# A second block's MLP up projection in channel order with the weights stationary, and two reordered places: the first chunk and the state-space roots

## The chip, the cores and the metric

The kernel runs on one core of a Trainium2 chip. The metric is device time in microseconds (us) from launch to the end of one execution; three runs of the kernel before gave 3005.98, 3007.11 and 3009.41, median 3007.11. About 0.2% (6 us) is the least difference that can be told from none.

The core has a matrix engine (PE; its weight loads are listed apart as PEld), a vector engine (DVE), an activation engine (ACT), GpSimd (POOL) and a queue engine (SP) that here issues the weight loads from memory. They run on their own and meet at semaphores.

## The reference, cut to what matters

256 tokens, width 2048, two blocks in fp32. The three places that the change touches:

```
proj = rmsnorm(h, g) @ w_in                       # first block: its first 512 columns are the "first chunk"
...
y = _ssd(...) + d_skip * xs;  y = y * silu(z)     # state space, 4 groups of 512 channels
y_ssm = rmsnorm(y.reshape(b, s, 4, 512), ssm_norm_g)   # one root per token and group
h = h + concat([y_ssm, y_att]) @ w_out
...
h = rms_norm(x, g_mlp)                            # second block's MLP, hidden width 8192
x = x + jnp.square(relu(h @ w_mlp_up)) @ w_mlp_down
return rms_norm(x, g_final)
```

The root 1/rms of a token is a positive factor r of its whole row, so square(relu(r * u)) is r * r * square(relu(u)).

## The kernel before, in words

**Weights.** All large products run through one stream of weights. A slab is 256 input rows by 512 output columns (two tiles of 128 x 512, 512 KB). SP loads slabs in order into a ring of four (`w_raw`); ACT rounds each to `w_hi` (fp32r, line 754), DVE forms the rest `w_lo = w_raw - w_hi` (line 1341). `hi_ready` and `lo_ready` count slabs; SP reloads a place once its `w_lo` is written, ACT overwrites `w_hi` once PE has counted the slab of four before in `slab_done`. Four slabs are a quad; `split(q, a, b)` on ACT and on DVE does slabs a to b of quad q.

**Products.** The activations are kept as channels x tokens, also in two parts (`a_hi`, `a_lo`; for the MLP's second product `m_hi`, `m_lo`). A 128x128 tile of them is the stationary operand, 512 weight columns are the moving one, and the result is 128 tokens x 512 columns in a bank of PSUM. A slab takes 12 matmuls of 512 columns: hi x hi, lo x hi (line 2137) and hi x lo (line 2142), for two weight tiles and two token tiles. A chunk is 512 output columns over all 2048 inputs: 8 slabs.

**Operands.** A new operand is turned on PE (line 2165, four 128x128 transposes per pair of channel tiles), rounded by ACT (`gained`, line 779, or `rounded_operand`, line 773) and its rest formed by DVE (`gained_rest`, line 1355, `rest_of_operand`, line 1347). The engines' orders are written out by hand: each block below is one engine's program.

**First chunk.** `first_chunk` on PE turns tile pairs 0 and 1, then for slab s turns pair s+1, waits for `a_lo` of pair s and runs slab s. ACT does pair s+1 ahead of the rounding of slab s (line 845 on). After the chunk comes `narrow`: 48 matmuls whose stationary operand has 32 columns and whose moving operand has 256 (lines 2213 to 2215). It waits for DVE's line 1469, which follows eight squares of ACT (line 763) and one small rounding (line 856).

**State-space groups.** In a loop over four groups POOL scales (lines 614 to 629), PE multiplies within and across chunks beside the slabs of the q, k, v chunks, and DVE makes the gated output in `z`. After the loop POOL computes all eight roots `ssm_rs` (lines 547, 548) and DVE normalizes `z` (line 1611); PE turns it beside the last chunk of q, k, v, in groups of pairs (0,1), (2), (3,4), (5), (6) ahead of slabs 3 to 7.

**MLP.** `w_mlp_up` is taken in 16 blocks of 512 hidden channels. Per block PE runs the up chunk of block j+1 into the banks of `pair[2]`, then `mlp_down` of block j (four chunks of two slabs). ACT and DVE scale the up chunk's result by r into `m_stage` (lines 784 and 1361), PE turns it to channel order (`mlp_channels`, line 2234, eight transposes into banks 6 and 7), ACT takes relu and its square (`m_relu` line 1277, `m_hi` line 1280), DVE the exact product `m_act` (line 2049) and the rest `m_lo` (line 2055), and DVE adds each down chunk to `h` (line 1413). The last block's relu to `m_lo` (lines 1299, 1301, 2084, 2088) stands between the last transposes and the last down product.

Of the kernel before, what the change touches and what calls it, by code (L numbers as in the profile page):

```python
# [192 lines left out]
def program(nc, wstream, small, const, out):  # L193

    ctx = ExitStack()
    with ctx:
# [27 lines left out]
        with ExitStack() as rows:  # L224
# [55 lines left out]
            with ExitStack() as part:  # L280
# [255 lines left out]
        def _(pool):  # L536
# [66 lines left out]
            for g in range(GROUPS):  # L603
# [22 lines left out]
                for t in range(TT):  # L626
# [3 lines left out]
                    if t == 0:  # L630
# [6 lines left out]
            inverse_root(ssm_rs[:].rearrange("p t g -> p (t g)"), ssm_ss[:].rearrange("p t g -> p (t g)"),  # L637
                         TT * GROUPS, 1.0 / NC, EPS, ssm_rstd)
# [108 lines left out]
        def _(act):  # L747
# [103 lines left out]
            split(Q_XBC + 1, QUAD - 1, QUAD)  # L851
# [2017 lines left out]
```

## Time and profile before

| | before |
|---|---|
| median of three runs | 3007.11 us |
| the profiled execution | 3011.07 us, its span 3009.0 us |
| PE busy | 2955.5 us, 98% |
| PEld busy | 2422.7 us, 81% |
| DVE busy | 2010.2 us, 67% |
| ACT busy | 1411.7 us, 47% |
| POOL busy | 322.5 us, 11% |
| mean granted clock of TensorE | 0.994 |

The page of the profile lists busy time per engine, the chain of work that ended last, and groups of instructions by line. The timeline lists instructions in order of time with their start, length and, in brackets, how long the engine had been idle and what released it.
### The profile page before, as it was taken

To read this page: it belongs to the slowest core of one execution; us is meant where nothing else is said; L and a number is where in the kernel's file an instruction comes from. 1 tells how busy PE (TensorE), PEld (TensorE's weight loads), DVE (VectorE), ACT (ScalarE), POOL (GpSimd) and SP (SyncE) were. 2 spreads that over 40 slices of the span, in tenths; PEclk is the share of its full clock that TensorE was granted. 3 is DMA by queue.
4 is the path that set the end of the run, shared out by engine and by line. 5 is a ranking of instruction groups with operands and counts; after the bars stand their busy time and mean duration, and the time that the engine had idled before them with its cause. 6 is when DMAs were issued, how large, how long until landed. Compare 5 with 4: busy or idle time off the path is not lost.

```text
span 3009.0 us, 43769 instructions
## 1 busy us (share of the span) xinstructions
PE 2955.5 (98%) x15191; PEld 2422.7 (81%) x15191; DVE 2010.2 (67%) x2615; ACT 1411.7 (47%) x1807; POOL 322.5 (11%) x276
## 2 busy tenths in 40 slices
PE   6999999999999999999999999999999999999998
PEld 5888877788888888887878877777888888888886
DVE  3765777756666777776668677777655666666665
ACT  4444445644444444445554554333545444444444
POOL 0001880000000000000000054443000000000000
PEclk8999999999999999999999999999999999999999
DMA  4555444456555555564565533333765565555554
GB/s 167 181 183 188 136 135 150 134 187 217 189 188 188 184 188 181 187 196 146 183 230 179 168 126 126 113 124 112 240 220 193 185 196 188 187 190 188 188 189 140
DMA packets 145142, 525.73 MB, mean 175 GB/s; under 512 B 16416, under 2 KB 17184, under 8 KB 144160
## 3 DMA queue, kind: packets, MB, share of 16 engines
q1 hardware_dynamic: 139760, 503.72, 51.6%
q0 software_dynamic: 1536, 11.78, 1.1%
q10 hardware_dynamic: 3760, 9.05, 0.9%
q8 instruction: 58, 0.95, 0.1%
q14 instruction: 28, 0.23, 0.0%
HBM read 516.09 MB, written 8.39 MB: 174 GB/s over the span
## 4 chain that ended last, share of the span: by engine, by line
PE 91%; DVE 3%; issue 2%; ACT 2%; POOL 1%; DMA 1%; DVEq 0%; ACTq 0%; POOLq 0%; SPq 0%
PE bank L2137 55%; PE bank L2142 27%; PE bank L2234 1%; DVE w_lo L1341 1%; ACT w_hi L754 1%; PE bank L2554 1%; PE bank L2165 1%; DMA w_raw<-weights 1%; PE bank L2583 0%; PE bank L2372 0%; PE bank L2305 0%; PE bank L2466 0%; PE bank L2316 0%; PE bank L2242 0%; DVE delta L1875 0%
## 5 line engine op out<-in xcount | busy, mean ns | idle before, releaser
L1341 DVE TENSOR_TENSOR w_lo<-w_raw,w_hi 128x1024 fp32r<-128x1024 f32 x952 | 1197.3, 1267 | 789.5 <-ACT w_hi L754 788.3
L754 ACT CAST w_hi<-w_raw 128x1024 fp32r<-128x1024 f32 x952 | 1000.1, 1052 | 1408.7 <-PE bank L2142 1394.9
L2137 PE MATMUL bank<-w_hi,a_hi 128*128 128x512 f32 x2816 | 1125.5, 400 | 16.5 <-ACT w_hi L754 14.6
L2137 PE MATMUL bank<-w_hi,a_lo 128*128 128x512 f32 x2816 | 1104.2, 392 | 0.0
L2142 PE MATMUL bank<-w_lo,a_hi 128*128 128x512 f32 x2816 | 761.4, 391 | 0.0
L2137 PEld LDWEIGHTS bank<-w_hi,a_hi 128*128 128x128 f32 x2816 | 531.8, 189 | 136.0 <-DVE a_lo L1355 13.0
L2142 PEld LDWEIGHTS bank<-w_lo,a_hi 128*128 128x128 f32 x2816 | 531.7, 189 | 112.8
L2137 PEld LDWEIGHTS bank<-w_hi,a_lo 128*128 128x128 f32 x2816 | 532.6, 189 | 107.1 <-issue 1.9
L2137 PE MATMUL bank<-w_hi,m_hi 128*128 128x512 f32 x496 | 193.5, 390 | 2.3 <-issue 2.3
L2137 PE MATMUL bank<-w_hi,m_lo 128*128 128x512 f32 x496 | 193.4, 390 | 0.0
L1413 DVE TENSOR_TENSOR h<-h,bank 128x512 f32<-128x512 f32 x236 | 151.1, 682 | 19.6 <-PE bank L2142 19.5
L2137 PE MATMUL bank<-w_hi,f_hi 128*128 128x512 f32 x352 | 138.8, 394 | 0.0
L553 POOL TENSOR_TENSOR rstd<-rstd,neg_half 128x2 f32<-128x2 f32 x6 | 4.8, 798 | 1240.9 <-DVE rstd L1370 1240.9
L2137 PE MATMUL bank<-w_hi,f_lo 128*128 128x512 f32 x352 | 137.1, 390 | 0.0
L2142 PE MATMUL bank<-w_lo,m_hi 128*128 128x512 f32 x496 | 133.5, 391 | 0.0
L2137 PEld LDWEIGHTS bank<-w_hi,m_hi 128*128 128x128 f32 x496 | 93.4, 188 | 21.9 <-issue 2.5
L2142 PEld LDWEIGHTS bank<-w_lo,m_hi 128*128 128x128 f32 x496 | 93.7, 189 | 19.6
L2137 PEld LDWEIGHTS bank<-w_hi,m_lo 128*128 128x128 f32 x496 | 93.4, 188 | 19.4
L2142 PE MATMUL bank<-w_lo,f_hi 128*128 128x512 f32 x352 | 94.2, 389 | 0.0
L2142 PEld LDWEIGHTS bank<-w_lo,f_hi 128*128 128x128 f32 x352 | 66.1, 188 | 13.9
L2137 PEld LDWEIGHTS bank<-w_hi,f_lo 128*128 128x128 f32 x352 | 66.1, 188 | 13.5 <-issue 0.2
L745 POOL TENSOR_TENSOR rstd<-rstd,neg_half 128x1 f32<-128x1 f32 x2 | 1.5, 746 | 704.6 <-DVE rstd L2099 704.6
(397 smaller groups left out, 2489.7 us busy)
## 6 DMA issues: line engine op xcount, KB each, us to landing
w_raw<-weights SPq DMA_DIRECT2D x952, 512.0 KB, 4.1
gate<-gate_st ACTq DMA_DIRECT2D x8, 512.0 KB, 3.9
h<-gate ACTq DMA_DIRECT2D x8, 512.0 KB, 4.7
gain<-gains POOLq DMA_DIRECT2D x3, 1024.0 KB, 6.9
h<-x_tok SPq DMA_DIRECT2D x4, 512.0 KB, 11.1
w_proj_sb<-w_proj POOLq DMA_DIRECT2D x1, 2048.0 KB, 9.8
h_rest<-h POOLq DMA_DIRECT2D x1, 2048.0 KB, 13.2
h<-h_rest POOLq DMA_DIRECT2D x1, 2048.0 KB, 9.6
```

The lines of the kernel that those rows point to most:

```text
L553: nc.gpsimd.tensor_tensor(rstd[:, n], rstd[:, n], neg_half[:, 0:TT], ALU.pow).then_inc(rstd_ready, 1)
L745: nc.gpsimd.tensor_tensor(rstd[:, N_OUT, t:t + 1], rstd[:, N_OUT, t:t + 1], neg_half[:, 0:1], ALU.pow).then_inc(rstd_ready, 1)
L754: nc.scalar.copy(w_hi[:, s, :], w_raw[:, s, :]).then_inc(hi_ready, 1)
L1341: V.tensor_tensor(w_lo[:, s, :], w_raw[:, s, :], w_hi[:, s, :].bitcast(F32), ALU.subtract).then_inc(lo_ready, 1)
L1413: V.tensor_tensor(h[:, t, col], h[:, t, col], pair[p][t][:], ALU.add).then_inc(pair_free[p], 1)
L2137: T.matmul(psum[t][:], left[:, t * P:(t + 1) * P], wh, start=start and j == 0 and n == 0, stop=False)
L2142: last = T.matmul(psum[t][:], products[j][0][:, t * P:(t + 1) * P], wl, start=False, stop=stop and j == SLAB_KT - 1)
L2165: last = T.transpose(bank[4 + i % 4][:, k * SEQ + t * P:k * SEQ + (t + 1) * P], src[:, t, (2 * i + k) * P:(2 * i + k + 1) * P], ident[:])
L2234: last = T.transpose(bank[first + ct // 2][:, (ct % 2) * SEQ + t * P:(ct % 2) * SEQ + (t + 1) * P], src[:, t, col0 + ct * P:col0 + (ct + 1 ...
L2554: last = T.matmul(out[r, r], left[:, r], right[:, r], start=True, stop=True)
```

## The change

It has three parts.

**First chunk.** ACT rounds slab s ahead of tile pair s+1, not behind it, and DVE's `gained_rest` follows suit. PE's order stays. ACT's order in this part before, from the first rounding of an operand (`a_hi`; `gain_col_sb` holds the norm's gains) on:

```order
L779 ACTIVATE a_hi<-bank,gain_col_sb 128x256 [waits tr_ready,gain_ready]
L779 ACTIVATE a_hi<-bank,gain_col_sb 128x256
L779 ACTIVATE a_hi<-bank,gain_col_sb 128x256 [waits tr_ready]
L779 ACTIVATE a_hi<-bank,gain_col_sb 128x256
L754 CAST w_hi<-w_raw 128x1024 [waits raw_loaded0]
L779 ACTIVATE a_hi<-bank,gain_col_sb 128x256 [waits tr_ready]
L779 ACTIVATE a_hi<-bank,gain_col_sb 128x256
L754 CAST w_hi<-w_raw 128x1024 [waits raw_loaded1]
```

The same place in the changed kernel:

```order
L782 ACTIVATE a_hi<-bank,gain_col_sb 128x256 [waits tr_ready,gain_ready]
L782 ACTIVATE a_hi<-bank,gain_col_sb 128x256
L757 CAST w_hi<-w_raw 128x1024 [waits raw_loaded0]
L782 ACTIVATE a_hi<-bank,gain_col_sb 128x256 [waits tr_ready]
L782 ACTIVATE a_hi<-bank,gain_col_sb 128x256
L757 CAST w_hi<-w_raw 128x1024 [waits raw_loaded1]
```

The rounding of slab 1 (`raw_loaded1`) stood behind the third tile pair and now stands behind the second.

**State-space roots.** POOL computes group g-1's two roots inside the loop at group g, between `xds` and the skip product; DVE normalizes group g-1 there. After the loop only group 3 is left, and PE turns one pair ahead of each of slabs 1 to 7. DVE's order behind the loop before (`z` is what is normalized, `a_lo` the rest of an operand, `w_lo` the rest of a slab):

```order
L1572 TENSOR_REDUCE qk_ss<-xs 128x8 [waits qk_sq] x2
L1611 SCALAR_TENSOR_TENSOR z<-z,ssm_rs,gain 128x512 [waits gain_loaded,ssm_rstd]
L1611 SCALAR_TENSOR_TENSOR z<-z,ssm_rs,gain 128x512
L1341 TENSOR_TENSOR w_lo<-w_raw,w_hi 128x1024 [waits hi_ready]
L1611 SCALAR_TENSOR_TENSOR z<-z,ssm_rs,gain 128x512 x2
L1341 TENSOR_TENSOR w_lo<-w_raw,w_hi 128x1024 [waits hi_ready]
L1611 SCALAR_TENSOR_TENSOR z<-z,ssm_rs,gain 128x512 x2
L1341 TENSOR_TENSOR w_lo<-w_raw,w_hi 128x1024 [waits hi_ready]
L1611 SCALAR_TENSOR_TENSOR z<-z,ssm_rs,gain 128x512 x2
L1347 TENSOR_TENSOR a_lo<-bank,a_hi 128x512 [waits a_hi_ready] x3
```

The same place now:

```order
L1575 TENSOR_REDUCE qk_ss<-xs 128x8 [waits qk_sq] x2
L1568 SCALAR_TENSOR_TENSOR z<-z,ssm_rs,gain 128x512 [waits ssm_rstd]
L1568 SCALAR_TENSOR_TENSOR z<-z,ssm_rs,gain 128x512
L1343 TENSOR_TENSOR a_lo<-bank,a_hi 128x512 [waits a_hi_ready]
L1337 TENSOR_TENSOR w_lo<-w_raw,w_hi 128x1024 [waits hi_ready]
L1343 TENSOR_TENSOR a_lo<-bank,a_hi 128x512 [waits a_hi_ready]
L1337 TENSOR_TENSOR w_lo<-w_raw,w_hi 128x1024 [waits hi_ready]
```

Six of the eight normalizing instructions left this place for the loop, two in each of groups 1 to 3.

**MLP.** The up chunk is computed with 128x128 tiles of the weights stationary and 256 tokens moving (`channel_chunk`), so it comes out in channel order. `m_stage` and `mlp_channels` are gone; relu reads banks 6 and 7 (for block 0 `pair[0]`) without r, and `ms_m` = r * r is applied where the down product is added to `h`. The relu of block j+1 moves to the end of its up chunk; the last block gets buffers of its own (`last_hi`, `last_lo`). PE's order at the end of a block before, where a down slab ends and the next block's up chunk begins:

```order
L2142 MATMUL bank<-w_lo,m_hi 128x512 [waits lo_ready]
L2142 MATMUL bank<-w_lo,m_hi 128x512 x3
L2234 MATMUL bank<-ident_sb,m_stage 128x128 [waits pair_free2]
L2234 MATMUL bank<-ident_sb,m_stage 128x128 x7
L2764 UNCONDITIONAL_BRANCH
L2764 ISA
L2132 ISA [waits pair_free2]
L2137 MATMUL bank<-w_hi,a_hi 128x512 [waits hi_ready]
L2137 MATMUL bank<-w_hi,a_lo 128x512
```

PE's order now, from the end of an up chunk to the start of the down product:

```order
L2735 MATMUL bank<-a_hi,w_hi 128x256
L2736 MATMUL bank<-a_lo,w_hi 128x256
L2739 MATMUL bank<-a_hi,w_lo 128x256 [waits lo_ready]
L2739 MATMUL bank<-a_hi,w_lo 128x256 x7
L2753 ISA [waits ff_lo]
L2117 ISA [waits pair_free0]
L2122 MATMUL bank<-w_hi,m_hi 128x512 [waits hi_ready]
L2122 MATMUL bank<-w_hi,m_lo 128x512
```

A slab of the up projection is 24 matmuls of 256 columns in place of 12 of 512, each with a weight load of 128 columns; the transposes are gone.

```diff
@@ ACT, first chunk @@
+            split(0, 0, 1, first=True)
+            for s in range(1, QUAD):
+                gained(TR_ATTN, C_ATTN, s)
+                split(0, s, s + 1, first=True)
             for s in range(QUAD):
-                gained(TR_ATTN, C_ATTN, s + 1)
-                split(0, s, s + 1, first=True)
-            for s in range(QUAD - 1):
-                gained(TR_ATTN, C_ATTN, QUAD + s + 1)
+                gained(TR_ATTN, C_ATTN, QUAD + s)
                 split(Q_XBC + 1, s, s + 1)
@@ POOL, in the loop over groups @@
                     pool.wait_ge(y_squared, TT * g)
+                    inverse_root(ssm_rs[:, :, g - 1], ssm_ss[:, :, g - 1], TT, 1.0 / NC, EPS, ssm_rstd)
@@ DVE, in the loop over groups @@
+                if g:
+                    ssm_normalize(g - 1)
@@ PE, last chunk of q, k, v @@
-                  between={3: lambda: tiles_of_y(0, 1), 4: lambda: tiles_of_y(2), 5: lambda: tiles_of_y(3, 4),
-                           6: lambda: tiles_of_y(5), 7: lambda: tiles_of_y(6)})
+                  between={i + 1: lambda i=i: tiles_of_y(i) for i in range(KT // 2 - 1)})
@@ PE, MLP @@
+            def channel_chunk(q, psum, ahead=None):
+                for n in range(KT // SLAB_KT):
+                    if ahead:
+                        ahead(n)
+                    u, s = q + n // QUAD, n % QUAD
+                    first, final = n == 0, n == KT // SLAB_KT - 1
+                    places = [(j, ct, psum[ct // 2][:, (ct % 2) * SEQ:(ct % 2 + 1) * SEQ], slice(j * NC + ct * P, j * NC + (ct + 1) * P))
+                              for j in range(SLAB_KT) for ct in range(NC // P)]
+                    pe.wait_ge(hi_ready, QUAD * u + s + 1)
+                    for j, ct, o, w in places:
+                        T.matmul(o, w_hi[:, s, w], a_hi[:, n * SLAB_KT + j], start=first and j == 0 and ct % 2 == 0, stop=False)
+                        T.matmul(o, w_hi[:, s, w], a_lo[:, n * SLAB_KT + j], start=False, stop=False)
+                    pe.wait_ge(lo_ready, QUAD * u + s + 1)
+                    for j, ct, o, w in places:
+                        last = T.matmul(o, w_lo[:, s, w], a_hi[:, n * SLAB_KT + j], start=False,
+                                        stop=final and j == SLAB_KT - 1 and ct % 2 == 1)
+                    last.then_inc(slab_done, 1)
...
             def mlp_block(j, between=None):
                 q = Q_MLP + 2 + 4 * j
-                chunk(q, 2, V_MLP + j, a_hi, a_lo, between=between)
+                channel_chunk(q, bank[6:8])
                 pe.wait_ge(ff_lo, N_FF + 2 * j + 2)
                 mlp_down(q + 2, U_MLP + 2 * j)
-                pe.wait_ge(pair_free[2], 2 * (V_MLP + j + 2))
-                mlp_channels()
@@ DVE, MLP @@
+            def add_block_to_h(p, col, tiles=range(TT)):
+                for t in tiles:
+                    V.scalar_tensor_tensor(h[:, t, col], pair[p][t][:], ms_m[:, t:t + 1], h[:, t, col], ALU.mult, ALU.add).then_inc(pair_free[p], 1)
```

## Rows read from the trace of the kernel before

**Rows 1.** The page: span, busy time by engine, chain that ended last by line.

```profile
span 3009.0 us, 43769 instructions
PE 2955.5 (98%) x15191; PEld 2422.7 (81%) x15191; DVE 2010.2 (67%) x2615; ACT 1411.7 (47%) x1807; POOL 322.5 (11%) x276
...
PE bank L2137 55%; PE bank L2142 27%; PE bank L2234 1%; DVE w_lo L1341 1%; ACT w_hi L754 1%; PE bank L2554 1%; PE bank L2165 1%; DMA w_raw<-weights 1%; PE bank L2583 0%; PE bank L2372 0%; PE bank L2305 0%; PE bank L2466 0%; PE bank L2316 0%; PE bank L2242 0%; DVE delta L1875 0%
```

**Rows 2.** Stretches: length, PE, PEld, DVE, ACT, POOL busy, clock, DMA share, GB/s.

```profile
16.50:59.50 43.00, 31.27 (x109) 23.87 (x107) 13.74 (x19) 16.32 (x35) 0.00 (x0) 0.80 0.35 118
...
46.98:50.39 3.41, 3.39 (x8) 2.73 (x9) 1.13 (x1) 0.00 (x0) 0.00 (x0) 0.50 0.34 91
...
2311.00:2348.00 37.00, 37.00 (x165) 30.65 (x164) 22.14 (x24) 15.35 (x15) 0.00 (x0) 1.00 0.61 186
```

**Rows 3.** Timeline, first chunk: start, length, engine, line, operation, idle before.

```profile
16.55 0.60 PE L2165 MATMUL bank<-ident_sb,h 128*128 128x128 f32 x4
17.19 0.84 ACT L779 ACTIVATE a_hi<-bank,gain_col_sb 128x256 fp32r<-128x256 f32 x2 [5.82 <-PE bank L2165]
17.92 1.04 ACT L754 CAST w_hi<-w_raw 128x1024 fp32r<-128x1024 f32 x1
...
19.11 0.47 PE L2137 MATMUL bank<-w_hi,a_hi 128*128 128x512 f32 x1 [1.95 <-ACT w_hi L754]
...
51.41 0.60 PE L2165 MATMUL bank<-ident_sb,h 128*128 128x128 f32 x4
...
60.96 0.31 PE L2213 MATMUL bank<-a_hi,w_hi 128*32 128x256 f32 x1 [1.31 <-DVE w_lo L1469]
```

**Rows 4.** DMA: first four slabs (issue line 493) to landing; all sixteen until 75 us.

```profile
L493 SPq DMA_DIRECT2D w_raw<-weights x4: 424/616/672, 1.5 to 4.0; - x4
...
DMA to landing us min/median/max: 8.8/10.0/11.3
...
w_raw<-weights SPq DMA_DIRECT2D x16, 512.0 KB, 4.3
```

**Rows 5.** Timeline of PE, last chunk of q, k, v beside the turned y.

```profile
424.14 1.07 PE L2142 MATMUL bank<-w_lo,a_hi 128*128 128x512 f32 x4
...
441.66 0.63 PE L2165 MATMUL bank<-ident_sb,z 128*128 128x128 f32 x4 [2.60 <-DVE a_lo L1347]
...
449.66 0.60 PE L2165 MATMUL bank<-ident_sb,z 128*128 128x128 f32 x4
...
452.85 0.60 PE L2165 MATMUL bank<-ident_sb,z 128*128 128x128 f32 x4
```

**Rows 6.** Timeline: PE at group 2 of the state space; a root of width 2 on POOL.

```profile
364.85 1.12 PE L2324 MATMUL bank<-work,b_tok 128*128 128x512 f32 x2 [0.95 <-POOL work L618]
...
2296.22 0.72 POOL L553 TENSOR_TENSOR rstd<-rstd,neg_half 128x2 f32<-128x2 f32 x1 [100.79 <-DVE rstd L1370]
```

**Rows 7.** Timeline of PE around the MLP's transposes: first, a middle and the last block.

```profile
2305.98 1.07 PE L2142 MATMUL bank<-w_lo,a_hi 128*128 128x512 f32 x4
...
2308.61 0.39 PE L2137 MATMUL bank<-w_hi,a_lo 128*128 128x512 f32 x1
...
2348.30 1.08 PE L2142 MATMUL bank<-w_lo,m_hi 128*128 128x512 f32 x4
...
2350.33 0.39 PE L2137 MATMUL bank<-w_hi,a_lo 128*128 128x512 f32 x1
...
2970.29 1.08 PE L2142 MATMUL bank<-w_lo,m_hi 128*128 128x512 f32 x4
...
2978.82 0.49 PE L2137 MATMUL bank<-w_hi,m_hi 128*128 128x512 f32 x1
```

**Rows 8.** Other shapes: the end of `narrow`; state-space matmuls 128x128; their weight loads.

```profile
66.47 0.28 PE L2215 MATMUL bank<-a_lo,w_hi 128*32 128x256 f32 x1
...
297.40 1.95 PE L2305 MATMUL bank<-before_sb,cv 128*128 128x128 f32 x16
...
L2305 PEld LDWEIGHTS bank<-before_sb,cv x128: 188/192/192, 297.2 to 405.7; 128*128 128x128 f32 x128
```

More of the change, by code:

```diff
@@ L1294, in _ @@
                 split(q + 4)
-            act.wait_ge(ff_t, N_FF + N_FF2)
+            with act.Fori(0, N_FF2 - 2) as j:
+                mlp_block(j)
+            mlp_block(N_FF2 - 2, last=True)
             j = N_FF2 - 1
-            for b in range(2):
-                half = slice(2 * b, 2 * b + 2)
-                nc.scalar.activation(m_relu[:, half].rearrange("p k s -> p (k s)"), bank[6 + b][:], ACT.Relu).then_inc(ff_silu, 1)
-                act.wait_ge(ff_silu, N_FF + 2 * j + b + 1)
-                nc.scalar.activation(m_hi[:, half], m_relu[:, half], ACT.Square).then_inc(ff_hi, 1)
@@ L2054, in mlp_gated, with mlp_down @@
                     dve.wait_ge(ff_hi, N_FF + 2 * j + b + 1)
-                    V.tensor_tensor(m_lo[:, half], m_act[:, half], m_hi[:, half].bitcast(F32), ALU.subtract).then_inc(ff_lo, 1)
-            def mlp_down(q, chunks=range(D // NC)):
-                for n in chunks:
+                    V.tensor_tensor(lo[:, half], m_act[:, half], hi[:, half].bitcast(F32), ALU.subtract).then_inc(ff_lo, 1)
+            def mlp_down(q):
+                for n in range(D // NC):
                     split(q + 1 + n // 2, 2 * (n % 2), 2 * (n % 2) + 2)
@@ L2089, in _ @@
-            mlp_down(N_QUADS - 4, range(D // NC - 1, D // NC))
+                dve.wait_ge(ff_lo, N_FF + 2 * j + 2)
+                mlp_act(j + 1, bank[6:8])
+                if last:
+                    mlp_lo(j + 1, last_hi, last_lo)
+                mlp_down(q + 2)
+            with dve.Fori(0, N_FF2 - 2) as j:
+                mlp_block(j)
+            mlp_block(N_FF2 - 2, last=True)
             def out_gain(t, n):
@@ L2771, in _ @@
                     pe.wait_ge(ff_lo, N_FF + 2 * (N_FF2 - 1) + s + 1)
-                    slab(N_QUADS - 2, 2 * n + s, [(m_hi[:, 2 * s + k], m_lo[:, 2 * s + k]) for k in range(SLAB_KT)],
+                    slab(N_QUADS - 2, 2 * n + s, [(last_hi[:, 2 * s + k], last_lo[:, 2 * s + k]) for k in range(SLAB_KT)],
                          pair[n], s == 0, s == 1)
@@ L2782, in _ @@
                             wh, wl = (x[:, i, k * NC:(k + 1) * NC] for x in (w_hi, w_lo))
-                            T.matmul(pair[n % 2][t][:], m_hi[:, tile, ts], wh, start=tile == 0, stop=False)
-                            T.matmul(pair[n % 2][t][:], m_lo[:, tile, ts], wh, start=False, stop=False)
-                            last = T.matmul(pair[n % 2][t][:], m_hi[:, tile, ts], wl, start=False, stop=tile == 3)
+                            T.matmul(pair[n % 2][t][:], last_hi[:, tile, ts], wh, start=tile == 0, stop=False)
+                            T.matmul(pair[n % 2][t][:], last_lo[:, tile, ts], wh, start=False, stop=False)
+                            last = T.matmul(pair[n % 2][t][:], last_hi[:, tile, ts], wl, start=False, stop=tile == 3)
                         last.then_inc(slab_done, 1)
```

143 lines of the change are left out of this document (59 added, 84 removed).

## The prediction

> **What bounds the kernel now.** I read the page first: PE is busy 98% of the span and the lines of the large products (2137 and 2142) are 82% of the chain that ended last [rows 1]. So PE's own pace decides, and a gain can only be a PE instruction removed, a faster one, or one of the few places where PE stands still. Then the stretches: in the MLP PE is full and DVE and ACT are at 22.1 and 15.4 of 37 us; 165 matmuls are listed in 37.00 us, of which two may hang over an edge, so a matmul of 512 columns takes 0.227 us and a slab of twelve 2.72 us. In the first chunk the granted clock is 0.80 in the mean, and one stretch of 3.41 us at 0.50 holds only 8 matmuls, 0.427 each [rows 2]. Last the timelines of PE at the three places that the change touches; the rows give where PE idles and what comes last there.
>
> **First chunk.** PE turns tile pair 2 at 16.55; ACT then does pair 2 (17.19) and only behind it slab 1's rounding (17.92), and PE starts slab 1 at 19.11, idle 1.95 us for that rounding [rows 3]. The same wait of about 2 us comes at slabs 1 to 7, and part of each slab runs at the lower clock. With the new order slab s is rounded before PE has turned pair s+1, so PE goes on at once. Beside it ACT needs 0.84 + 1.04 us per slab [rows 3], much less than PE. A slab with four transposes ahead takes 452.85 - 449.66 = 3.19 us at full clock [rows 5]. Pair 7 would be turned at 16.55 + 5 x 3.19 = 32.5 instead of 51.41. From there to `narrow` it took 60.96 - 51.41 = 9.55 us [rows 3], a chain on ACT and DVE that is unchanged but for one rounding (1.0) that now lies ahead of pair 7: 8.5, so `narrow` starts at 41.0, 19.9 earlier. What is late next is this chain: PE ends slab 7 at 16.55 + 6 x 3.19 + 2.72 = 38.4 and idles 2.6 us, not 1.3. Idling 1.31 us there cost no clock; 1.95 us at the slabs did. A stretch at 0.50 does half its 3.41 us of work, 1.7 us; I take half of that, 0.8. The data are there: the first four slabs, issued by 4.0 us, land within 11.3 us of issue, before 16; a later one lands some 4.3 us after issue [rows 4] and is asked for three slabs (9.6 us) ahead. Result -19.1, between -15 (the clock still falls twice, one landing late) and -19.9.
>
> **State-space roots.** PE ends slab 0 at 424.14 + 4 x 0.227 = 425.05 and turns pair 7 at 452.85 [rows 5]; in between it waits for the normalized `z`, once 2.60 us for the rest of an operand, and runs a stretch at the lower clock. With one pair turned ahead of each of slabs 1 to 7, pair 7 comes at 425.05 + 7 x 3.19 = 447.4: -5.5. DVE's rests and slabs (two short instructions a slab) fit in 3.19 us. The price is in the loop: POOL gets a root of width 2, 0.72 us [rows 6], and a scaling with its hand-over of some 0.3, three times. In group 2 PE already waits 0.95 us for POOL [rows 6], so there POOL's 1.0 us is on the path; in groups 1 and 3 POOL itself waits for DVE later. Cost 1.0, between 0 and 3. The six normalizing instructions in the loop are hidden by DVE's waits for ACT's roundings. Result -4.5, between -2.5 and -5.5.
>
> **MLP, what is removed.** In block 0, PE's last slab before the transposes ends with 4 matmuls from 2305.98; the second matmul after them should start 5 x 0.227 later, at 2307.11, and starts at 2308.61: 1.50. In a middle block 2350.33 - (2348.30 + 1.13) = 0.90, 14 times: 12.6. At the last block the first matmul of the second down slab would come at 2970.29 + 16 x 0.227 = 2973.92 and comes at 2978.82: 4.90, the wait for relu to `m_lo` with the lower clock behind it [rows 7]. With `last_hi` that work lies beside the previous down product. Sum -19.0. In return no wait is added that PE reaches: relu of block j+1 ends some microseconds after its up chunk, and its banks are needed again only after a down product of eight slabs. DVE's adds gain a factor but keep their shape, and each of ACT and DVE loses an instruction per block; with DVE busy 22.1 of 37 us [rows 2] this is hidden. If that cover were gone, DVE's two products ahead of the down product's slabs would cost PE up to 1.3 us a block.
>
> **MLP, what is added.** 16 up chunks of 96 matmuls of 512 columns become 16 x 192 = 3072 of 256, and 1536 more weight loads of 128 columns. The trace has no such matmul with such a load. The nearest rows: `narrow`, the same type and 256 moving columns, but loads of 32: 48 matmuls from 60.96 to 66.47, 5.51 / 47 = 0.1172 each [rows 3, 8]. And the state-space products, where loads of 128 columns and 128x128 matmuls run at (1.95 - 0.28) / 15 = 0.111 (0.28 is the listed length of a last one, as at 66.47) although each load is listed with 0.192 [rows 8]: the listed length is no pace, and a load needs at most 0.111. I take the larger of the two paces, 0.1172: (2 x 0.1172 - 0.2267) x 1536 = +11.9. Ends: half the old pace, 0.1133, gives 0; the listed 0.192 as a pace gives +230.
>
> The Trainium skill (TensorE: Matmul & The Clock Gate, section Back-to-back issue gap) puts a lone matmul at N / 2.4 + 2.5 ns; 256 columns would be 109 ns, against 216 for 512, and the doubling would cost about 4 us. The trace does not agree: 117 and 227 ns.
>
> **Sum.** -19.1 - 4.5 - 19.0 + 11.9 = -30.7. The profiled execution took 3011.07 (span 3009.0 and 2.1 around it), 4.0 over the median of the runs: 2980.4 on its scale, 2976.4 on the median's. Forecast 2976.
>
> **Rivals.**
>
> Slower: the load is not hidden under a matmul of 256 columns. A 512-column matmul lasts long enough to cover a load; a 256-column one lasts about as long as the load, and if the load had to wait for the matmul's end, 1536 more loads at 0.111 would stand in the open: +170 in place of +11.9, 3135. The kernel gets slower from a pace of 0.1172 + 30.7 / 3072 = 0.127 on. For it: nothing in the trace shows both at once in fp32r. Against: `before_sb,cv` runs load and matmul of nearly equal length at 0.111, so they overlap [rows 8]. Chance 6%. The Trainium skill (same page, section The mechanism) says that a load overlaps a matmul in flight only when the two use different row groups, which speaks for this rival; the trace disagrees, as loads of all 128 rows run beside matmuls of all rows.
>
> A dearer pace: what a 256-column matmul takes beyond 256 / 2.4 GHz = 0.1067, namely 0.0105 [rows 3, 8], comes on top of the load's 0.111: 0.1215, so +25 in place of +11.9: 2990. For it: load and matmul are near a tie. Against: at the tie in `before_sb,cv` nothing is added. Chance 15%.
>
> The first chunk gives half: the clock falls in stretches as now (0.80 in the mean) or ACT's order makes another wait. For it: the clock before 16 us is low, and PE idles before `narrow`. Against: no idle is left between slabs. -9.5 in place of -19.1: 2986. Chance 11%.
>
> A cheaper pace: 256 columns cost half of 512, 0.1133: 2964.5. For it: the weight load is hidden in both. Against: `narrow`. Chance 6%.
>
> The change does nothing: the removed waits come back at the next wait of each place. Against: the waits are for work that is off PE, and PE is full behind each. About 3%.
>
> **How the numbers follow.** My forecast has 59%, own range 2969 to 2984. The range that should hold 8 in 10 reaches from the cheaper pace to the dearer one with a small loss elsewhere: 2965 to 2994. About 0.2% (6 us) is what can be told from no change; slower by that needs the first rival, 6%; within it are the last rival and one in a hundred of the others, 4%; faster 90%.
>
> **What would show each step.** First chunk: no wait of PE for `w_hi` after slab 0, `narrow` starting near 41, clock near 1.00 from 16 us on; wrong if slabs stay 5 us or more apart. Roots: PE turns `z` four transposes at a time every 3.19 us without a wait, and the wait for POOL in group 2 grows by about 1. MLP: up slabs of 24 matmuls in 2.81 us; a block period of 21.8 + 22.5 = 44.3 us, against 22.5 + 21.8 + 0.90 = 44.4 before; no gap at the last block. If an up slab takes over 3.05 us, the gain is gone.

## The result, and the profile after

The changed kernel took 2991.41 us, the median of five runs (2990.52 to 2995.49), for 3007.11 before: a ratio of 0.9949, 95% interval 0.9934 to 0.9963. The gain of 15.7 us is clear of the noise and is half of the 30.7 forecast; 2991.4 lies in the range, and is close to the 2990 of the rival "a dearer pace". The profiled execution took 2991.41, with a span of 2989.6 for 3009.0 before. The profiled execution of the kernel before was 4.0 over its median and that of the changed kernel is its median, so the traces differ by some 4 us more than the medians do.

The page of the changed kernel (span; busy time by engine; the chain that ended last, by line), which answers to [rows 1]:

```profile
span 2989.6 us, 46565 instructions
PE 2949.5 (99%) x16599; PEld 2481.6 (83%) x16599; DVE 2008.3 (67%) x2600; ACT 1402.6 (47%) x1791; POOL 327.3 (11%) x282
PE bank L2122 46%; PE bank L2127 23%; PE bank L2739 4%; PE bank L2736 4%; PE bank L2735 4%; DVE w_lo L1337 1%; PE bank L2219 1%; PE bank L2538 1%; PE bank L2150 1%; ACT w_hi L757 1%; DMA w_raw<-weights 1%; POOL work L633 1%; PE bank L2567 0%; PE bank L2356 0%; POOL xs L601 0%
```

PE still bounds the kernel. The new lines 2735, 2736 and 2739 are the up projection in channel order. Next PE's timeline of the changed kernel (start, length, line, what, idle before it and its releaser), in the first chunk and at the turned `z`, for [rows 3, 5]:

```profile
16.47 0.60 PE L2150 MATMUL bank<-ident_sb,h 128*128 128x128 f32 x4
19.67 0.60 PE L2150 MATMUL bank<-ident_sb,h 128*128 128x128 f32 x4
...
32.48 0.60 PE L2150 MATMUL bank<-ident_sb,h 128*128 128x128 f32 x4
...
41.08 0.31 PE L2198 MATMUL bank<-a_hi,w_hi 128*32 128x256 f32 x1 [2.51 <-DVE w_lo L1463]
...
407.73 0.60 PE L2150 MATMUL bank<-ident_sb,z 128*128 128x128 f32 x4
...
430.03 0.60 PE L2150 MATMUL bank<-ident_sb,z 128*128 128x128 f32 x4
...
434.36 0.63 PE L2341 MATMUL bank<-ident_sb,qkv 128*128 128x128 f32 x4 [0.99 <-DVE a_lo L1343]
```

Slabs with their transposes come every 3.20 us without a wait, pair 7 at 32.48 (forecast 32.5), `narrow` at 41.08 (41.0). Pair 7 of `z` follows pair 0 by 22.30, seven times 3.19. The stretches of the changed kernel (length; PE, PEld, DVE, ACT, POOL busy; clock, DMA share, GB/s) answer to [rows 2]:

```profile
16.50:42.00 25.50, 22.99 (x117) 18.81 (x116) 14.46 (x27) 17.76 (x37) 1.24 (x1) 1.00 0.59 206
...
2330.00:2351.00 21.00, 21.00 (x177) 21.00 (x177) 11.58 (x12) 8.63 (x10) 0.00 (x0) 1.00 0.58 189
```

The clock is full in the first chunk, where it was 0.80. In the up chunk the loads (PEld) are busy all 21.00 us, as the matmuls are: a thing that no row of before showed. The timeline of PE there, an up chunk between two down products, and the start of the last down product, for [rows 7]:

```profile
2329.00 0.28 PE L2735 MATMUL bank<-a_hi,w_hi 128*128 128x256 f32 x1
2329.12 0.28 PE L2736 MATMUL bank<-a_lo,w_hi 128*128 128x256 f32 x1
2329.24 0.28 PE L2735 MATMUL bank<-a_hi,w_hi 128*128 128x256 f32 x1
...
2330.92 1.12 PE L2739 MATMUL bank<-a_hi,w_lo 128*128 128x256 f32 x8
2331.88 0.28 PE L2735 MATMUL bank<-a_hi,w_hi 128*128 128x256 f32 x1
...
2348.20 1.12 PE L2739 MATMUL bank<-a_hi,w_lo 128*128 128x256 f32 x8
...
2352.04 0.40 PE L2122 MATMUL bank<-w_hi,m_hi 128*128 128x512 f32 x1
...
2955.58 1.07 PE L2127 MATMUL bank<-w_lo,m_hi 128*128 128x512 f32 x4
2956.48 0.39 PE L2122 MATMUL bank<-w_hi,last_hi 128*128 128x512 f32 x1
```

Every matmul of the up chunk starts 0.1200 us after the one before it: a slab of 24 takes 2.88, a chunk of 192 takes 2352.04 - 2329.00 = 23.04. The forecast had 0.1172, 2.81 and 22.5. Before, chunk and transposes took 22.66. At the last block the wait is gone.

To see where the rest went I cut the traces at the starts of the same matmuls, from the first transpose of `h` to PE's last matmul, and took each stretch's length less that of the kernel before. The labels e2 to e10 are the experiments below (e10 leaves out half of the up projection). One stretch of 3.41 us at the half clock (granted clock 0.50) costs up to 1.7, and such stretches come and go between executions, so a lone difference of 1.3 to 1.7 that another kernel shows without its cause is put down to them. In the fourth column no kernel changes anything but the first three up slabs (+0.5 with the channel order), yet it reads +0.5 to +3.7: half-clock stretches and waits between 1545 and 1790 us differ from one execution to the next.

| us, less before | to `narrow` | to `b_tok`, group 2 | to pairs of q, k, v | to the last pair of the MLP's operand | to the first down | 14 blocks | last but one down, to the last | last down | sum |
|---|---|---|---|---|---|---|---|---|---|
| after | -19.9 | +0.4 | -3.0 | +1.7 | +0.5 | +5.5 | -3.3 | -1.6 | -19.6 |
| e2 token MLP | -19.4 | +1.8 | -3.0 | +0.7 | 0.0 | 0.0 | 0.0 | 0.0 | -19.8 |
| e3 channel MLP | +0.6 | -0.1 | -1.6 | +2.5 | +0.5 | +5.5 | -3.3 | -1.6 | +2.6 |
| e4 early last | -20.4 | +0.5 | -3.0 | +3.1 | 0.0 | 0.0 | -0.4 | -1.7 | -21.9 |
| e5 first chunk | -19.7 | 0.0 | -0.1 | +1.5 | 0.0 | 0.0 | 0.0 | -1.6 | -19.8 |
| e6 roots | +0.2 | +0.5 | -3.0 | +2.1 | 0.0 | 0.0 | 0.0 | -1.6 | -1.7 |
| e7 root later | -20.2 | +2.4 | -4.3 | +0.5 | 0.0 | 0.0 | -0.4 | -1.7 | -23.6 |
| e8 add first | -20.4 | +0.6 | -3.0 | +1.0 | 0.0 | 0.0 | -2.4 | -1.7 | -25.9 |
| e9 both | -20.0 | +2.5 | -4.2 | +0.7 | 0.0 | 0.0 | -2.4 | -1.7 | -25.1 |
| e10 half | -19.2 | +1.9 | -3.2 | +3.7 | -1.5 | -12.2 | -3.3 | -1.6 | -35.5 |

### The profile page after: what moved, and what is told of

Its sections match the earlier page's. It is cut to its first block, busy times and chain, and to the rows that moved or that the text cites. A ratio compares the mean times of both kernels' runs of the same rounds, so it can differ in the third digit from the quotient of the medians.

```text
span 2989.6 us, 46565 instructions
## 1 busy us (share of the span) xinstructions
PE 2949.5 (99%) x16599; PEld 2481.6 (83%) x16599; DVE 2008.3 (67%) x2600; ACT 1402.6 (47%) x1791; POOL 327.3 (11%) x282
## 3 DMA queue, kind: packets, MB, share of 16 engines
q0 software_dynamic: 1536, 11.78, 1.1%
## 4 chain that ended last, share of the span: by engine, by line
PE 89%; POOL 3%; DVE 3%; issue 2%; ACT 2%; DMA 1%; DVEq 0%; ACTq 0%; SPq 0%; POOLq 0%
PE bank L2122 46%; PE bank L2127 23%; PE bank L2739 4%; PE bank L2736 4%; PE bank L2735 4%; DVE w_lo L1337 1%; PE bank L2219 1%; PE bank L2538 1%; PE bank L2150 1%; ACT w_hi L757 1%; DMA w_raw<-weights 1%; POOL work L633 1%; PE bank L2567 0%; PE bank L2356 0%; POOL xs L601 0%
## 5 line engine op out<-in xcount | busy, mean ns | idle before, releaser
L2122 PE MATMUL bank<-w_hi,a_hi 128*128 128x512 f32 x2304 | 921.1, 400 | 4.7 <-ACT w_hi L757 2.8
L2122 PE MATMUL bank<-w_hi,a_lo 128*128 128x512 f32 x2304 | 900.1, 391 | 0.0
L2127 PE MATMUL bank<-w_lo,a_hi 128*128 128x512 f32 x2304 | 622.0, 390 | 0.0
L2127 PEld LDWEIGHTS bank<-w_lo,a_hi 128*128 128x128 f32 x2304 | 433.2, 188 | 91.5
L2736 PE MATMUL bank<-a_lo,w_hi 128*128 128x256 f32 x1024 | 251.2, 283 | 0.0
L2735 PE MATMUL bank<-a_hi,w_hi 128*128 128x256 f32 x1024 | 251.2, 283 | 0.0
L2736 PEld LDWEIGHTS bank<-a_lo,w_hi 128*128 128x128 f32 x1024 | 196.5, 192 | 0.6
L2735 PEld LDWEIGHTS bank<-a_hi,w_hi 128*128 128x128 f32 x1024 | 196.5, 192 | 0.6
L2739 PE MATMUL bank<-a_hi,w_lo 128*128 128x256 f32 x1024 | 143.7, 283 | 0.0
L2739 PEld LDWEIGHTS bank<-a_hi,w_lo 128*128 128x128 f32 x1024 | 132.1, 192 | 0.0
```

The source lines that it names most:

```text
L2122: T.matmul(psum[t][:], left[:, t * P:(t + 1) * P], wh, start=start and j == 0 and n == 0, stop=False)
L2127: last = T.matmul(psum[t][:], products[j][0][:, t * P:(t + 1) * P], wl, start=False, stop=stop and j == SLAB_KT - 1)
L2735: T.matmul(o, w_hi[:, s, w], a_hi[:, n * SLAB_KT + j], start=first and j == 0 and ct % 2 == 0, stop=False)
L2736: T.matmul(o, w_hi[:, s, w], a_lo[:, n * SLAB_KT + j], start=False, stop=False)
L2739: last = T.matmul(o, w_lo[:, s, w], a_hi[:, n * SLAB_KT + j], start=False, stop=final and j == SLAB_KT - 1 and ct % 2 == 1)
```

## The experiments

Each code cut shows the main lines only. Those of e2 and e10 are against the changed kernel, that of e4 against e2, those of e7 and e8 against e4.

### e1: the pace of a matmul by itself

Nineteen bursts of 96 fp32r matmuls, each of this form, with m stationary and n moving columns (m also sets the number of rows of the result):

```
+ for i in range(N):
+     b, o = places(kind, n)[i % len(places(kind, n))]
+     last = T.matmul(bank[b][0:m, o], stationary(kind, i, m), a_hi[:, i % 2, 0:n], start=False, stop=False)
```

> This kernel leaves the whole computation out: it loads x, and TensorE runs 19 bursts of 96 fp32r matmuls, twice over, each burst with its own number of stationary columns (32 to 128), moving columns (128 to 512) and places in PSUM. Read is the time from one start to the next within a burst. Theory (a matmul of this kind costs its columns and a fixed part): the changed kernel showed 120.0 ns for 256 columns and 226.7 for 512, both behind a load of 128 columns, which is 0.417 ns a column and 13.3 ns fixed; so 384 columns take 173, 192 take 93, and 128 columns are bound by the load at 108 to 112 (the transposes' spacing). First rival (the length of the load sets the part on top): 256 columns behind 32 stationary columns take 117.3 as in the narrow projection, 64 and 96 lie between, 512 behind 32 take less than 226.7. Second rival (where the result goes sets it: half a bank, the same place twice, changing banks): behind 128 stationary columns the bursts of 256 columns with other places in PSUM differ by 2 ns or more among themselves, and the one that stays in one place of one bank takes 117 or less. The theory gives them all 120.0.

Each row below is one burst: count, length of a matmul, start of the first and of the last. The pace is the difference of the two over 95. The form at the end gives the stationary columns (128*128, 128*96, ...) and the moving ones.

```profile
L75 PE MATMUL bank<-a_hi,w_hi x96: 389/389/389, 47.7 to 69.2; 128*128 128x512 f32 x96
...
L79 PE MATMUL bank<-a_hi,w_hi x96: 333/334/346, 69.4 to 85.9; 128*128 128x384 f32 x96
...
L87 PE MATMUL bank<-a_hi,w_hi x96: 283/283/283, 97.6 to 109.0; 128*128 128x256 f32 x96
...
L107 PE MATMUL bank<-a_hi,w_hi x96: 244/275/277, 154.4 to 164.9; 128*128 128x128 f32 x96
...
L111 PE MATMUL bank<-a_hi,w_hi x96: 274/278/307, 165.1 to 176.1; 128*96 128x256 f32 x96
...
L115 PE MATMUL bank<-a_hi,w_hi x96: 276/276/276, 176.2 to 187.0; 128*64 128x256 f32 x96
...
L119 PE MATMUL bank<-a_hi,w_hi x96: 276/276/276, 187.1 to 197.9; 128*32 128x256 f32 x96
...
L135 PE MATMUL bank<-a_hi,w_hi x96: 220/222/224, 258.9 to 264.6; 128*64 128x128 f32 x96
...
L147 PE MATMUL bank<-a_hi,w_hi x96: 283/283/283, 282.0 to 293.4; 128*128 128x256 f32 x96
```

From the exact starts: 256 moving columns take 120.0 ns behind 128 stationary columns, 116.3 behind 96, 113.3 behind 64 and behind 32. The place in PSUM makes no difference: one place, two halves of a bank, two banks, four places, eight banks (line 147) and the same weights each time all give 119.9 to 120.0, and the kernel's own order, two matmuls in turn on one place, 120.5. Behind 128 stationary columns 512 moving ones take 226.7, 384 take 173.6, 192 take 111.5 and 128 take 111.3; 128 behind 64 take 60.0.

So the number of stationary columns matters, as the first rival says, and the theory of a fixed part of 13.3 falls, since with a short load 256 columns take 6.7 less; so does the second rival. A load of 128 columns paces PE at 111 ns, a stream of 256 columns at 113.3, and the two together give not the larger but 120.0. With 384 columns nothing is left of it: 173.4 behind 32, 173.6 behind 128. The first rival was wrong in detail: 117.3 behind 32 columns, taken from `narrow` [rows 8], came out as 113.3, the same as behind 64, and 512 behind 32 took 231.7 (behind 64: 229.9) and not less than 226.7. Neither has been explained. A burst with fewer stationary columns also writes fewer rows of the result, so the length of the load is not told apart from that; for the load speaks that at 384 moving columns both give the same.

### e2: the token-order MLP with the two reordered places

```
-            channel_chunk(Q_MLP, pair[0], late_tiles)
+            late_chunk(TR_MLP, h_chunk(U_WO2), Q_MLP, 0, U_MLP)
...
-                channel_chunk(q, bank[6:8])
+                chunk(q, 2, V_MLP + j, a_hi, a_lo, between=between)
                 pe.wait_ge(ff_lo, N_FF + 2 * j + 2)
                 mlp_down(q + 2, U_MLP + 2 * j)
+                pe.wait_ge(pair_free[2], 2 * (V_MLP + j + 2))
+                mlp_channels()
```

> The changed kernel with the MLP of the kernel before, that is, the first chunk and the state-space roots changed and nothing else. Theory (the MLP change is what came out dearer than forecast, by the pace of 0.1200 us for a matmul of 256 columns): the MLP begins 21.2 us earlier than in the kernel before, as in the changed kernel, and then takes as long as in the kernel before: 3007.1 - 21.2 = 2985.9, so 5 to 6 us faster than the changed kernel; blocks every 44.43 us. Rival (the first chunk and the roots gave less than is seen, and the MLP gave the forecast -7.1): 2991 + 7 = 2998.

2988.35 (2986.46 to 2991.22), ratio to the kernel before 0.9930 (0.9916 to 0.9943). The kernel before took 3009.2 beside it, so the gain is 20.8, as the theory had it (21.2), where the rival had 9. The changed kernel's own ratio, 0.9949 (0.9934 to 0.9963), overlaps with it; the table tells them apart in the MLP's columns, where e2 has 0.0 and the changed kernel +1.2, with 0.5 more in the column ahead of them (the first three up slabs, 72 matmuls).

### e3: the channel-order MLP alone

The eight pieces of the diff in the MLP, without those in the first chunk and at the roots.

> The kernel before with the MLP change alone. Theory (pace 0.1200): the ends read from the two traces, block 0 with the first chunk +1.0, 14 blocks of 44.82 for 44.43 = +5.5, the last block -4.9, together +1.6: 3008.7, no difference that the timing can tell. Forecast's own terms C and D: -7.1, 3000.0. Rival (what comes before the MLP interacts with it, so that the parts do not add): neither, and the first chunk or the middle of the trace differs from that of the kernel before by over 0.5 us.

3012.32 (3008.09 to 3013.36), ratio 1.0007 (0.9998 to 1.0016): no gain, and perhaps a small loss. In the trace its MLP columns equal those of the changed kernel to 0.01: +0.5, +5.5, -3.3, -1.6. The last of these need not be the MLP's, since e5 and e6 show it too. So the MLP change costs about 0.5 + 0.5 + 5.5 - 3.3 = +3.2 (+1.6 if the 1.6 is counted to it), where the forecast had -7.1. The last column is the half-clock stretch behind the wait before the last down product: it stands in two of the four traces with that wait (the kernel before and e2) and in none of the seven without it, so what its removal is worth lies between 0 and 1.6.

### e4: token order, and the last operand early

```
-                mlp_down(q + 2, U_MLP + 2 * j)
-                pe.wait_ge(pair_free[2], 2 * (V_MLP + j + 2))
-                mlp_channels()
+                mlp_down(q + 2, U_MLP + 2 * j, turned if last else None)   # turned(): that wait and the transposes
+                if not last:
+                    turned()
...
+                if last:                     # ScalarE, ahead of its splits of the down slabs
+                    mlp_relu(j + 1, last_hi)
...
-            mlp_down(N_QUADS - 4, range(D // NC - 1))
+            mlp_down(N_QUADS - 4, range(1))
+            mlp_gated(N_FF2 - 1, last_hi, last_lo)
+            mlp_down(N_QUADS - 4, range(1, D // NC))
```

> As the run with the token-order MLP, and the operand of the last block is turned, squared and split into buffers of its own while the down projection of the block before it runs (its transposes stand between the first and the second of the four column pairs there). Theory (the last block's gain in the changed kernel comes from this early operand and not from the channel order): the wait of 2.54 us before the last down projection goes, and with it the half clock that followed it, together -4.0 against the token-order run: 2981.9, the fastest of all. Rival (without the channel order the operand is late, since it needs transposes and a staging copy as well): TensorE stands in the down projection of the last block but one or ahead of the last, and the time is that of the token-order run, 2986, or above.

2988.81 (2987.07 to 2991.15), ratio 0.9931 (0.9918 to 0.9945), the same as e2 within the noise: a miss. In the trace its end is 2.1 shorter than e2's, and 1.7 of that is the half-clock stretch that e2 has and e4 has not; the fourth column took 2.4 more. The wait before the last down product is gone, and a new one stands in the down product before it. The timeline of e4, all engines:

```profile
2935.85 1.09 ACT L1272 ACTIVATE m_relu<-bank 128x512 f32<-128x512 f32 x2 [4.63 <-PE bank L2215]
2936.82 1.15 ACT L1275 ACTIVATE last_hi<-m_relu 128x512 fp32r<-128x512 f32 x2
2937.87 2.94 ACT L756 CAST w_hi<-w_raw 128x1024 fp32r<-128x1024 f32 x3
2938.95 2.36 DVE L1336 TENSOR_TENSOR w_lo<-w_raw,w_hi 128x1024 fp32r<-128x1024 f32 x2 [6.39 <-ACT w_hi L756]
...
2941.22 1.28 DVE L1408 TENSOR_TENSOR h<-h,bank 128x512 f32<-128x512 f32 x2
...
2942.56 0.50 PE L2118 MATMUL bank<-w_hi,m_hi 128*128 128x512 f32 x1 [1.26 <-DVE h L1408]
```

DVE stands 6.39 us for `w_hi`, which ACT rounds only behind relu and square, and DVE's addition to `h` stands in its queue behind that. PE needs the bank that this addition frees, and stands idle 1.26 us.

### e5 and e6: the first chunk alone, the roots alone

The two pieces of the diff in the first chunk; the six at the roots.

> The kernel before with the first chunk's change alone. Forecast's term A: -19.1. The two traces together gave -19.5 behind the narrow projection (41.08 us for 60.96, less 0.4 lost further on). Theory (the parts add): 3007.1 - 19.5 = 2987.6, the narrow projection begins at 41.1, and the half-clock stretches in the first 50 us are gone. Rival (what the first chunk wins is lost again in the state-space stretch, where GpSimd is as late as TensorE): -17 or less gained, 2990 or above, with new waits for GpSimd between 300 and 400 us.

2991.09 (2990.07 to 2995.45), ratio 0.9944 (0.9930 to 0.9958): 17.7 for 19.5 expected, within the interval. The time alone would also suit the rival (2990 or above); the trace decides. `narrow` begins at 41.2, and at the matmul of group 2 shown below (345.11 for 364.85) all of it is still there, with the old wait of 0.95 and no new one. The rival falls.

> The kernel before with the state-space roots' change alone. Forecast's term B: -4.5. The two traces together gave -3.0 (-22.4 at 600 us, less -19.5). Theory (parts add): 3004.1; the last pair of z is turned 4.5 to 5.5 us earlier relative to what stands before it, and 1.5 is lost to the root in group 2. Rival (the GpSimd wait belongs to the earlier arrival from the first chunk, not to the root): -4.5 or more, 3002.6 or below, and no new wait in groups 1 to 3.

3008.26 (3004.24 to 3011.47), ratio 0.9996 (0.9987 to 1.0005): by the timing no difference. In the trace +0.5 - 3.0 = -2.5, and 1.6 of that is a half-clock stretch of the kernel before that e3, with the old roots and the old waits, has not got. What the roots bring is then 0.9 where that stretch does not come and 2.5 where it does. The new wait for GpSimd is there without the new first chunk, so it belongs to the root. PE at `b_tok` in groups 2 and 3, of e5 (roots as before) and of e6 (new):

```profile
345.11 1.12 PE L2322 MATMUL bank<-work,b_tok 128*128 128x512 f32 x2 [0.95 <-POOL work L618]
376.16 1.13 PE L2322 MATMUL bank<-work,b_tok 128*128 128x512 f32 x2
```

```profile
365.50 1.13 PE L2314 MATMUL bank<-work,b_tok 128*128 128x512 f32 x2 [0.92 <-POOL work L618]
398.13 1.13 PE L2314 MATMUL bank<-work,b_tok 128*128 128x512 f32 x2 [0.92 <-POOL work L618]
```

From group 2 to group 3 it takes 31.05 us with the old roots and 32.63 with the new ones. Summed from group 1 on, the loop is some 2.6 longer, for the 1.0 that the forecast charged once. The slack was gone: before, POOL stands 2.36 us for DVE at 340.04 and 2.37 at 403.55, and in the changed kernel it has no such wait between 290 and 407 us.

### e7: the root later on GpSimd

```
                 if g:
                     pool.wait_ge(y_squared, TT * g)
-                    inverse_root(ssm_rs[:, :, g - 1], ssm_ss[:, :, g - 1], TT, 1.0 / NC, EPS, ssm_rstd)
...
                         qk_scaled(g, 0)
+                if g:
+                    inverse_root(ssm_rs[:, :, g - 1], ssm_ss[:, :, g - 1], TT, 1.0 / NC, EPS, ssm_rstd)
```

> As the run with the token-order MLP and the early last operand, with the root of a group's norm moved on GpSimd from ahead of the skip product to behind the two segment products. Theory (the root lengthens the chain that TensorE waits for between 345 and 385 us): up to 1.5 us less, 2980.4 for the 2981.9 expected of that run. Rival (GpSimd has no slack in a group at all, so its order does not matter): the same within 0.3 us; the waits move to the next group.

2987.26 (2987.03 to 2988.74), ratio 0.9930 (0.9916 to 0.9943) for 0.9931 of e4: no difference in the timing, whose interval of some 4 us to either side could not show the 1.5 of the theory either. The waits of PE in the loop (five of 0.3 to 0.93 in e4) have become one (the timeline of e7):

```profile
344.98 1.90 POOL L620 TENSOR_TENSOR work<-work,ds 128x512 f32<-128x512 f32 x1
...
346.93 2.08 PE L2306 MATMUL bank<-work,b_tok 128*128 128x512 f32 x2 [3.46 <-POOL work L620]
```

At its end the clock fell for 3.41 us (0.50 from 346.4), and in e9 it did again at the same place. By the table the two columns of the loop sum to -1.9 in e7 and -2.5 in e4: without the stretch e7 would be up to 1.1 better, and the stretch takes that back. The rival has it right that the waits move and the time stays, but that GpSimd has no slack at all is not shown.

### e8 and e9: the addition first

```
-            mlp_down(N_QUADS - 4, range(1))
+            dve.wait_ge(slab_done, QUAD * (N_QUADS - 4) + 2)
+            add_to_h(0, slice(0, NC))
             mlp_gated(N_FF2 - 1, last_hi, last_lo)
+            split(N_QUADS - 3, 0, 2)
```

> As the run with the early last operand (e4), but in the last block but one VectorE adds the first column pair to h and prepares the last operand before it splits the next two slabs, not behind them. There TensorE stood 1.65 us before the third column pair, for this addition, which had stood behind w_lo and so behind ScalarE's relu and square. Theory (the wait moved, and the order on VectorE is what holds it): the wait is gone, the stretch from the first to the last down projection is 3.2 to 3.3 us less less 0.9 for the transposes, so 1.6 to 2.0 under e4: 2987 for e4's 2988.8 and before's 3009. Rival (ScalarE's split is late by relu and square, whatever VectorE does): the wait stays at 1 us or more and moves to the slab's w_lo: 2988.8.

2984.80 (2982.80 to 2986.22), ratio 0.9920 (0.9906 to 0.9933). The column "last but one down" goes from -0.4 to -2.4, by the 2.0 expected, and PE does not stand in it. The timeline of e8:

```profile
2932.92 1.04 PE L2217 MATMUL bank<-ident_sb,m_stage 128*128 128x128 f32 x8
2933.73 0.68 DVE L1408 TENSOR_TENSOR h<-h,bank 128x512 f32<-128x512 f32 x1
2934.00 1.08 ACT L1272 ACTIVATE m_relu<-bank 128x512 f32<-128x512 f32 x2 [4.63 <-PE bank L2217]
...
2935.83 1.29 DVE L2045 TENSOR_TENSOR last_lo<-m_act,last_hi 128x512 fp32r<-128x512 f32 x2
2936.01 2.94 ACT L756 CAST w_hi<-w_raw 128x1024 fp32r<-128x1024 f32 x3
2937.10 4.75 DVE L1336 TENSOR_TENSOR w_lo<-w_raw,w_hi 128x1024 fp32r<-128x1024 f32 x4
```

The addition now fills the time in which DVE had stood. ACT's rounding is as late as in e4 and costs nothing: the first of those slabs is rounded by 2937.1, and PE takes it up at 2939.28. The rival falls. e8 is the fastest of the complete kernels together with e9; its interval ends (0.9933) just below where that of the changed kernel begins (0.9934), so by the timing alone its lead over the changed kernel is barely shown, and the table's columns carry it.

> As e8, with the root later on GpSimd as in e7. Theory (e7's profile: from the first segment products to the operand of the queries, keys and values, the stretches sum to 1.8 us less than in the kernel before, with one half-clock stretch inside; without it some 3.4 less, against 2.4 with the root ahead): 1.0 under e8. Rival: e7's three waits of 0.7 to 1.3 us return at another place: the same as e8 within 0.3 us.

2984.55 (2984.07 to 2986.63), ratio 0.9920 (0.9906 to 0.9933), the same as e8. The timing cannot tell the theory's 1.0 from none. In the trace the loop's two columns sum to -1.7, for -2.4 in e8, with a half-clock stretch at 347.0 inside that e8 has not: as in e7, the stretch behind the one long wait takes back what the order gains.

### e10: half of the stationary columns

```
-psum[ct // 2][:, (ct % 2) * SEQ:(ct % 2 + 1) * SEQ], slice(j * NC + ct * P, j * NC + (ct + 1) * P)
+psum[ct // 2][0:P // 2, (ct % 2) * SEQ:(ct % 2 + 1) * SEQ], slice(j * NC + ct * P, j * NC + ct * P + P // 2)
```

> The changed kernel, with 64 stationary columns for 128 in every matmul of the channel-order up projection; the same number of matmuls, each of 256 columns. It leaves half of that projection's channels uncomputed. Theory (the load of 128 columns is what makes 120.0 ns of a matmul of 256 columns, and a load of 64 is hidden, as in the bursts alone: 113.3): 3072 times 6.7 ns = 20.5 us less than the changed kernel, 2973 beside 3009 for the kernel before, blocks every 43.5 us for 44.82. Rival (in the full kernel something else makes the 120.0: the other engines' traffic, or the change of tile at each matmul): the blocks stay within 0.3 us of 44.82 and the time at 2993.

2971.66 (2970.45 to 2975.48), ratio 0.9875 (0.9859 to 0.9890): 37.1 under the kernel before, where the changed kernel is 15.7 under it. The timeline of e10 in an up chunk:

```profile
2331.28 0.28 PE L2735 MATMUL bank<-a_hi,w_hi 128*64 128x256 f32 x1
2331.39 0.28 PE L2736 MATMUL bank<-a_lo,w_hi 128*64 128x256 f32 x1
...
2332.64 1.07 PE L2739 MATMUL bank<-a_hi,w_lo 128*64 128x256 f32 x8
...
2335.36 1.07 PE L2739 MATMUL bank<-a_hi,w_lo 128*64 128x256 f32 x8
```

A slab of 24 takes 2335.36 - 2332.64 = 2.72, or 0.1133 a matmul, and a block 43.55 for 44.82. With the same order, number of matmuls, waits and other engines, 64 stationary columns for 128 take off the 6.7 ns in the full kernel as in the bursts, so the rival falls. They halve the load and the rows of the result together; no run parts the two. The loads are listed as busy all the time here too (19.00 of 19.00 us), so their busy share does not tell whether they hold PE up. 0.1133 is the pace at which two matmuls of 256 columns would cost what one of 512 does.

## Why the prediction was half right

The direction was right, and so was what was said of the first chunk and of the waits that go. The MLP's new order, though, loses where it was to gain 7.1, and one term, its pace, carried most of the miss. By the prediction's own steps, in the trace:

- **First chunk**, forecast -19.1: measured -19.9 in the changed kernel and -19.7 alone (e5). Right, the chain behind pair 7 and PE's longer idle time before `narrow` (2.51 for 2.6) included. The 0.8 charged for the clock was not needed in this execution, but the risk is real: e2 and e10 have a stretch at 0.50 there (from 40.9 and 41.4), with `narrow` at 213 ns a matmul in it, and lose 1.4 to 1.5 (+1.8 and +1.9 in the second column for +0.4).
- **State-space roots**, forecast -4.5: measured -2.6. The part at the turned `z` is there: pairs every 3.19 us with no wait. The price in the loop was mis-sized, some 2.6 and not 1.0: "in groups 1 and 3 POOL itself waits for DVE later" failed. POOL's 1 us a group reached PE in group 3 as well (e6), while the wait in group 2 did not grow (0.82 for 0.95), and PE waits 0.99 behind the last slab, for 0.62 before. Of the gain, 1.6 hung on a half-clock stretch that need not be there (e3).
- **MLP, what is removed**, forecast -19.0: 1.50 in block 0 and 0.90 in each of 14 blocks were right. (With the measured pace, block 0 should be 384 x 0.1200 - 192 x 0.2267 - 1.50 = +1.1 longer, and is +1.0; a block 23.04 + 21.78 - 44.43 = +0.4, and is +0.4.) The last block gave 4.9 in the trace, as forecast, but only 3.3 of it for certain: the half clock behind the wait was counted as its sure consequence, and it is missing in e5 and e6, which have the same wait.
- **MLP, what is added**, forecast +11.9: measured 3072 x 0.1200 - 1536 x 0.2267 = +20.4. **This is the step that failed**: "I take the larger of the two paces, 0.1172". Each bound was nearly right by itself (by e1 0.1113 for the load and 0.1133 for the stream, which the forecast had at 0.1172 from `narrow`), but this load and this stream do not quite hide each other: together they take 0.1200, and the larger of the two is no estimate. The rival that added something at the tie had 0.1215 and +25. The forecast held against it that at the tie of `before_sb,cv` nothing is added [rows 8]. That row is of another type (fp32, 128 moving columns) and was no evidence for fp32r with 256; in e1 128 moving columns of fp32r take 0.1113 behind 128 stationary ones and 0.0600 behind 64, so there the load alone sets the pace and nothing is near a tie. Whether the fp32 row is such a case no run shows.
- **The slower rival** did not come: the load is hidden but for 6.7 ns. (The upper end that the forecast gave, +230, should read (2 x 0.192 - 0.2267) x 1536 = +242, and the block before is 21.8 + 21.8 + 0.90 = 44.4, not 22.5 + 21.8 + 0.90; neither enters the sum.) The pace of 0.127 from which the whole change would lose was not reached; but the MLP part alone, worth -7.1 in the forecast, is +3.2. Its own turning point, 0.1172 + 7.1 / 3072 = 0.1195, was never worked out, and 0.1200 is beyond it.

The forecast was -30.7 and the trace has -19.6. The miss of 11.1 is 8.5 for the pace (20.4 - 11.9), 1.9 for the roots, 1.2 for the stretch between them and the MLP, and 0.3 for down products of 21.79 us and not 21.77, less 0.8 at the first chunk. The 1.2 is shown by e5 as well (+1.5), which changes nothing there; 1.0 of it lies at a half-clock stretch at 1549 us that the kernel before has not. From there to the 15.7 of the medians it is the 4.0 by which the profiled execution of the kernel before lay over its median; in later runs its medians were 3008.8 to 3009.2, so some of that gap is chance. So it is in part luck that the time comes within 1.4 us of the dearer rival's 2990: that rival's own pace, 0.1215, is too dear by 4.6 us.

What the change brought was the first chunk (e5: ratio 0.9944 alone), a little at the roots, and the early operand of the last block. The channel order gave back 6.5 us (+0.5, +0.5 and +5.5). The version without it and with the two others (e8) took 2984.80, ratio 0.9920.

## What to carry to other kernels

Where a change cuts matmuls in two, measure the pace at exactly the new pair of load and stream lengths before counting on a hidden load; when the two are close, add to the larger. Judge each part of a change by its own break-even pace, not by that of the sum. When work is put into a full pipeline, look at what stands behind it in each engine's queue: e4 lost 2.0 us to one addition that could have gone first.

## What the runs showed of the hardware

- A load of 128 columns with a stream of 256 (fp32r): 120.0 ns, above both 111.3 (128 moving columns behind the same load) and 113.3 (256 behind 64 or 32 stationary columns). At 384 columns nothing of it is seen (173.6 for 173.4), and the place in PSUM has no effect at 256 (119.9 to 120.5).
- The starts are 113.3 for 256 moving columns, 60.0 for 128, 173.4 for 384 and 226.7 for 512: as if a long matmul were pieces of at most 256 columns (113.3 + 60.0 = 173.3; 2 x 113.3 = 226.7). That is a reading of four numbers; 512 behind 64 or 32 stationary columns (229.9, 231.7) does not fit it, and no run tested it.
- The half clock is not a fixed price of a wait. In the kernel before, stretches of 3.41 us at 1.2 GHz began at 442.9, behind a wait of 2.60, and at 2975.6, behind one of 2.26; e3, with the same wait before the first, and e5 and e6, with the same wait before the second, had none there. At the wait of 2.51 before `narrow` it fell in e2 and e10 and not in the changed kernel; at the wait of 3.46 us in e7 and e9 it fell both times.
- `narrow` runs at 117.2 ns [rows 3, 8], where the same shapes alone run at 113.3. What makes the difference is open.
